# Last SwiGLU of a two-layer diffusion trunk on one core: two weight units multiply the residual sums before they are normalised

## The chip, the cores and the metric

One core of a Trainium2 chip runs the whole program. The metric is the device time of one execution in microseconds (us), the median over runs. Three runs of the kernel before stand at 1689.14, 1692.32 and 1695.26 us.

## The reference

Two layers work on 256 latent tokens and 256 context tokens of width 1024. Each layer is a half-step SwiGLU, a token mixer and another half-step SwiGLU. Every sub-layer scales and shifts its input by conditioning (adaLN), and every result is normalised after the residual sum:

```python
def mod_input(z, mm, slot):
    return z * (1.0 + mm[:, 3 * slot + 1]) + mm[:, 3 * slot]

def gated_post_norm(z, y, mm, slot, g, b):
    return layer_norm(DEEPNORM_ALPHA * z + mm[:, 3 * slot + 2] * y, g, b)

def swiglu(h, w1, w2):
    gate, up = jnp.split(h @ w1, 2, axis=-1)
    return (jax.nn.silu(gate) * up) @ w2
```

The mixer of the second (odd) layer is attention with 8 query heads. Behind it only the 256 latent tokens are needed, so the last SwiGLU works on 256 columns. This case is about the place between the two: output projection of the attention, layer norm, modulation, first product (w1) of the last SwiGLU. With z the residual sums, mu their mean over the features and r the inverse deviation, one column block of that product is sum over features of w * ((z - mu) * r * s + t), where s and t join the norm's gain and bias with the modulation. It can also be written as r * (w . (s z) - mu * (w . s)) + w . t, and this is what the change does for two blocks.

## The kernel before, in words

Features lie on the partitions in KC = 8 chunks of 128, tokens along the free axis. Every float32 product is made of three float32r products: weight and input are each split into a high and a low part, and high x high, low x high and high x low are added in one PSUM bank.

**Units.** The weights stream through the kernel as units of 128x1024 (512 KB), all numbered in one order. SyncE loads unit n into a ring of RING = 7 buffers `raw`, and may do so once TensorE has used up unit n - 6 (`load_unit`). ScalarE makes the high part in `w_hi` (`split_hi`, line 832; a ring of 6), VectorE the low part in `w_lo` (`split_lo`, line 1277), written over the raw buffer of the unit before. TensorE counts finished units in the semaphore `w_used`. ScalarE and VectorE have no queue of their own for this: where the program order puts `split_to(n)`, there all units up to n - 1 are split, in between their other work. Usually they are AHEAD = 4 units or so in front of TensorE.

**Output projection of the attention** (`odd_mixer`, eight units `o_out`). When TensorE has finished block c, VectorE adds it to the residual `hz` (line 1362) and adds the result to `sum1` (line 1373; for chunk 0 a copy, line 1370). ScalarE squares chunk c - 1 (line 891), and GpSimd adds the squares of chunks 1 to 6 to `sum2` (line 767). Both splitters split one unit per block in between.

**Norm 4** (`one_norm(4)`, that is `norm_sums` and `norm_spread`). TensorE turns `sum1` and `sum2` into one sum per token by products with one column (lines 2176, 2181, 2186) and spreads the sum of the residuals over all partitions in bank 5 (line 2189). VectorE makes the inverse deviation in fifteen small steps on two columns (`norm_step`, lines 1384 to 1411), the last two of which write it as a diagonal. TensorE spreads it in bank 4 (line 2195). Then VectorE goes chunk by chunk through `normalise`: `centre` (line 1420), `scale` (line 1429), and `lower` (line 1440), which makes the low part of the new input from what ScalarE has made in `apply_norm`: the high part `a_hi` (line 869) and the unrounded input `tmp_b` (line 872).

**First product of the last SwiGLU** (`ffn(3)`). 22 units make one half of the hidden width: a gate unit and an up unit for each of HH = 11 hidden steps; then come eight w2 blocks of two units, and the second half the same. Call the 22 units of the first half u0 to u21. Before, `first_four` (line 2230) takes u0 to u3 together, chunk by chunk as the input comes. The units behind are `paired_unit` (lines 2119 and 2120): high weight against both input parts in one product of 512 columns, then low weight against 256 columns. Unit u goes to one of banks 0 to 3 and waits (`bank_read`) until the unit four before it was read. In `hidden_step`, ScalarE applies SiLU to the gate (line 936, or 930 in a paired step, where lines 927 and 932 first copy the other half of the bank aside), VectorE multiplies (line 1530, or 1522 behind the adds of lines 1512 and 1516), ScalarE writes the high part (line 942) and VectorE the low part (line 1533). Line 881 (`keep`) scales the residual in between. A hidden step splits two units: one ahead of the product, one behind the high part.

Of the kernel before, what the change touches and what calls it, by code (L numbers as in the profile page):

```python
# [101 lines left out]
def paired_step(fi, half, j):  # L102

    return FFNS[fi][3] < T and (half == 1 or j >= 2)
# [124 lines left out]
def make_plan():  # L229
# [11 lines left out]
    def ffn(fi):  # L241
        layer, f = FFNS[fi][:2]
        for half in range(2):
            p.mark(("w1", fi, half))
            for j in range(HH):
                m = (fi * 2 + half) * HH + j
# [112 lines left out]
    "gate_rest", "gate_exp", "gla_ops", "hy_mid", "hy_read", "zf_ready", "att_even", "att", "att_read", "att_kept", "att_masked",  # L359
    "kst_turned", "kst_read", "ds", "ds_read", "state_ready", "g_read", "o_lower", "o_done", "o_sq",  # L360
    "o_root", "o_scaled", "o_turned", "gla_out", "z_turned", "zt_read",
    "dft", "dft_read", "spec_mixed", "spec_out", "skip_made", "idft", "idft_read", "cat", "cat_hi", "cat_ready",
# [7 lines left out]
def hybrid_trunk(nc, x_t, par_d, w1_d, w2_d, ada_d, ew_d, ev_d, eo_d, ow_d, ov_d, oo_d, gu_d,  # L370
# [4 lines left out]
    with ExitStack() as ctx:  # L375
# [108 lines left out]
        out_lo = [put(f"out_lo{i}", [P, UCOL], F32R, at=X + (52 + 4 * i) * K) for i in range(3)]  # L484
        osqr = put("osqr", [P, TC, GH * GDV], at=X + 56 * K)
# [261 lines left out]
        @block.gpsimd  # L747
        def _(pool):
            g = nc.gpsimd
            g.memset(scolp[:], 0.0).then_inc(s["zeroed"], 1)  # L750
            g.memset(ident[:], 0.0).then_inc(s["ones_made"], 1)
            pool.wait_ge(s["ones_made"], 1)
            g.affine_select(out=ident[:], in_=ident[:], compare_op=ALU.not_equal, fill=1.0, base=0,
                            pattern=[[-1, P]], channel_multiplier=1).then_inc(s["ones_made"], 1)
            g.memset(ones[:], 1.0).then_inc(s["ones_made"], 1)
            g.memset(fh[:], 1.0).then_inc(s["ones_made"], 1)

            def add_squares(m):
# [27 lines left out]
            pool.wait_ge(s["gate_rest"], 4)  # L786
# [11 lines left out]
        def _(act):  # L798
# [94 lines left out]

            def norm_inputs(m, nu):
# [24 lines left out]
            def ffn(fi):  # L919
                nt = FFNS[fi][3]  # L920

                def hidden_step(n, m, j):

                    act.wait_ge(s["w_used"], n + 1)
                    if paired_step(fi, half, j):
# [22 lines left out]
                for half in range(2):  # L948
# [5 lines left out]
                    for j in range(HH):  # L954
                        hidden_step(n0 + 2 * j, m0 + j, j)
# [53 lines left out]
            def even_mixer():  # L1009
# [17 lines left out]
                for e in range(4):  # L1027
                    act.wait_ge(s["gate_rest"], e + 1)
# [89 lines left out]
                for h in range(GH):  # L1118
# [3 lines left out]
                    A.copy(a_hi[:, YC + h, :], go[:, h, :]).then_inc(s["cat_hi"], 1)  # L1122
                for c in range(YC):
                    act.wait_ge(s["cat"], c + 1)
                    A.copy(a_hi[:, c, :], yt[:, c, :]).then_inc(s["cat_hi"], 1)
# [6 lines left out]
            def odd_mixer():  # L1132
# [121 lines left out]
        def _(dve):  # L1254
# [187 lines left out]

            def normalise(m, nu, j0):
# [40 lines left out]
                else:  # L1484
                    for i in range(NORM_STEPS):
                        norm_step(m, 0, i)
                    if m < 5:
                        split_to(nu + 4)
# [3 lines left out]
                    for c in range(KC):  # L1492
# [6 lines left out]
                        if m < 5 and c >= 1:  # L1499
                            lower(m, 0, c - 1)  # L1500
                    if m < 5:
                        lower(m, 0, KC - 1)

            def ffn(fi):
                _, _, _, nt, adas = FFNS[fi]

                def hidden_step(n, m, j, pieces):

                    if paired_step(fi, half, j):
# [8 lines left out]
                        if j < HH - 1:  # L1518
# [4 lines left out]
                                        ALU.mult).then_inc(s["hraw_ready"], 1)  # L1523
                    else:
# [14 lines left out]
                for half in range(2):  # L1539
# [12 lines left out]
                    for j in range(HH):  # L1552
                        hidden_step(n0 + 2 * j, m0 + j, j, pieces(j))
# [185 lines left out]
            def even_mixer():  # L1739
# [12 lines left out]
                for e in range(4):  # L1752
# [5 lines left out]
                    else:  # L1758
# [6 lines left out]
                                    ALU.subtract).then_inc(s["gate_rest"], 1)  # L1765
# [166 lines left out]
                def lower_cat(c, at, src):  # L1932

                    dve.wait_ge(s["cat_hi"], at + 1)
                    V.tensor_tensor(a_lo[:, c, :], src, a_hi[:, c, :].bitcast(F32), ALU.subtract)\
                        .then_inc(s["cat_ready"], 1)
# [43 lines left out]
            def odd_mixer():  # L1980
# [120 lines left out]
        def _(pe):  # L2101
# [160 lines left out]

            def paired_unit(n, j):
# [6 lines left out]
            def ffn(fi):  # L2270
                _, _, _, nt, adas = FFNS[fi]
                n_sub = SUB_OF_FFN[fi]
                for half in range(2):
                    n0, j0 = plan.base[("w1", fi, half)]
                    m0 = (2 * fi + half) * HH
                    if fi == half == 0:
                        pass
                    elif half == 0:
                        first_four(n_sub - 1, n0, j0, (0, 1)[:nt // SEQ])
# [7 lines left out]
                    for u in range(4, 2 * HH):  # L2287
# [180 lines left out]
            def even_mixer():  # L2468
# [188 lines left out]
                for pair in ((0, 1), (2, 3)):  # L2657
# [3 lines left out]
                    for at, k in enumerate(ks[:YC]):  # L2661
                        pe.wait_ge(s["cat_ready"], at + 1)
                        for u in pair:
                            four_out(k, u)
                for at, k in enumerate(ks[YC:KC - 2]):
                    pe.wait_ge(s["cat_ready"], YC + at + 1)
                    for u in range(4):
                        four_out(k, u)
                pe.wait_ge(s["cat_ready"], KC)
# [179 lines left out]
            one_norm(4)  # L2849
# [104 lines left out]
```

## Time and profile before

| | |
|---|---|
| runs, median (lowest to highest) | 1692.32 us (1689.14 to 1695.26) |
| the profiled execution's own time | 1695.77 us |
| its span | 1694.0 us |
| TensorE busy | 1667.0 us, 98% of the span |
| VectorE, ScalarE, GpSimd busy | 1182.8, 700.7, 72.7 us |
| last product of the attention's output projection | 1482.62 us |
| first product of the last SwiGLU | 1490.94 us |
| start of its first paired unit u4 | 1504.82 us |

Times within the trace are microseconds from the start of the span. The difference between the execution's own time and its span (1.77 us) lies around the span. In a view in order of time a row gives start, duration, engine, line, operation, tiles and, in square brackets, how long the engine stood idle before it and what released it. VectorE and ScalarE start an operation some 0.1 us before the one before it is shown as ended, so the cost of an operation in a queue is the distance between two starts.

### The profile page before, as it was taken

The page shows a single profiled execution, that of the slowest core. Times are in us where ns is not written, and L with a number is a line of the kernel's source. Part 1 is how long each engine was busy: PE and PEld are TensorE (multiplying, and loading weights), DVE is VectorE, ACT ScalarE, POOL GpSimd, SP SyncE. Part 2 cuts the span into 40 slices and gives each one's busy share as a digit, 9 for nine tenths or more (in the row PEclk, how much of TensorE's full clock was granted, in tenths as well). Part 3 has the DMA queues.
Part 4 walks back from the last instruction along what each step waited for, and adds up shares of the span by engine and source line. Part 5 has one row for each costly group of instructions (what it writes and reads, how often), then busy time and mean ns, then how long its engine had stood idle before and what let it go on. Part 6 is the DMA issues. An engine that isn't in the chain of part 4 may idle for free. (4 is left out here: it accounts for less than half of the span.)

```text
span 1694.0 us, 23629 instructions
## 1 busy us (share of the span) xinstructions
PE 1667.0 (98%) x9147; PEld 1404.5 (83%) x9147; DVE 1182.8 (70%) x1868; ACT 700.7 (41%) x1141; POOL 72.7 (4%) x62
## 2 busy tenths in 40 slices
PE   9999999999999999999999999999999999989997
PEld 6788888889877898888888898888888888878886
DVE  5577948978686866778533476778466687776767
ACT  3442242225645437422222246322323277665453
POOL 1000000001000020000000110000000110200001
PEclk9999999999999999999999999999999999989998
DMA  9665546632321232555322334554465342245653
GB/s 314 249 209 174 173 153 220 208 95 83 114 79 52 74 125 83 198 174 160 120 96 81 92 118 149 199 169 148 161 222 190 98 143 69 83 140 163 210 165 111
DMA packets 87094, 248.39 MB, mean 147 GB/s; under 512 B 8900, under 2 KB 24997, under 8 KB 86982
## 3 DMA queue, kind: packets, MB, share of 16 engines
q1 hardware_dynamic: 86504, 245.98, 44.8%
q8 instruction: 73, 1.20, 0.3%
q0 software_dynamic: 256, 0.46, 0.1%
q10 hardware_dynamic: 222, 0.43, 0.1%
q14 instruction: 39, 0.32, 0.1%
HBM read 245.79 MB, written 1.05 MB: 146 GB/s over the span
## 5 line engine op out<-in xcount | busy, mean ns | idle before, releaser
L1277 DVE TENSOR_TENSOR w_lo<-raw,w_hi 128x1024 fp32r<-128x1024 f32 (+2 forms) x337 | 380.5, 1129 | 154.9 <-ACT w_hi L832 148.3
L2104 PE MATMUL bank<-a_both,w_hi 128*128 128x512 f32 (+1 forms) x1200 | 462.2, 385 | 2.7 <-DVE w_lo L1277 1.4
L2105 PE MATMUL bank<-a_both,w_lo 128*128 128x512 f32 (+1 forms) x1200 | 460.2, 383 | 0.0
L2106 PE MATMUL bank<-a_both,w_hi 128*128 128x512 f32 (+1 forms) x1200 | 460.1, 383 | 0.0
L832 ACT CAST w_hi<-raw 128x1024 fp32r<-128x1024 f32 (+2 forms) x337 | 319.8, 955 | 161.0 <-DMA raw<-in_dram 157.7
L2104 PEld LDWEIGHTS bank<-a_both,w_hi 128*128 128x128 f32 x1200 | 225.5, 188 | 49.3 <-issue 2.3
L2106 PEld LDWEIGHTS bank<-a_both,w_hi 128*128 128x128 f32 x1200 | 225.5, 188 | 44.4
L2105 PEld LDWEIGHTS bank<-a_both,w_lo 128*128 128x128 f32 x1200 | 225.6, 188 | 43.8
L1295 DVE SCALAR_TENSOR_TENSOR acc<-ada,scol,acc 128x1024 f32<-128x1024 f32 x189 | 234.9, 1280 | 8.9 <-DMA ada<-in_dram 7.0
L2104 PE MATMUL bank<-h_both,w_hi 128*128 128x512 f32 (+1 forms) x473 | 183.5, 388 | 0.0
L2106 PE MATMUL bank<-h_both,w_hi 128*128 128x512 f32 (+1 forms) x473 | 182.9, 387 | 0.0
L2105 PE MATMUL bank<-h_both,w_lo 128*128 128x512 f32 (+1 forms) x473 | 182.8, 387 | 0.0
L942 ACT CAST h_both<-tmp_b 128x512 fp32r<-128x512 f32 (+1 forms) x88 | 49.9, 567 | 315.3 <-DVE tmp_b L1530 287.9
L1362 DVE SCALAR_TENSOR_TENSOR hz<-bank,acol,hz 128x256 f32<-128x256 f32 x136 | 61.3, 479 | 88.7 <-PE bank L2106 88.2
L767 POOL TENSOR_TENSOR sum<-sum,sq 128x256 f32<-128x256 f32 (+1 forms) x41 | 63.0, 1538 | 1339.4 <-ACT sq L891 1339.2
L2119 PE MATMUL bank<-a_both,w_hi 128*128 128x512 f32 x320 | 113.2, 399 | 0.0
L936 ACT ACTIVATE tmp_a<-bank 128x512 f32<-128x512 f32 (+1 forms) x68 | 40.1, 589 | 169.0 <-PE bank L2106 161.5
L2104 PEld LDWEIGHTS bank<-h_both,w_hi 128*128 128x128 f32 x473 | 88.8, 188 | 18.2
L2106 PEld LDWEIGHTS bank<-h_both,w_hi 128*128 128x128 f32 x473 | 88.8, 188 | 18.1
L2105 PEld LDWEIGHTS bank<-h_both,w_lo 128*128 128x128 f32 x473 | 88.8, 188 | 17.9
L1533 DVE TENSOR_TENSOR h_both<-tmp_b,h_both 128x512 fp32r<-128x512 f32 (+1 forms) x88 | 55.1, 626 | 55.7 <-ACT h_both L942 55.7
L1530 DVE TENSOR_TENSOR tmp_b<-tmp_a,bank 128x512 f32<-128x512 f32 (+1 forms) x68 | 46.1, 678 | 64.9 <-PE bank L2106 64.7
(338 smaller groups left out, 2248.6 us busy)
## 6 DMA issues: line engine op xcount, KB each, us to landing
raw<-in_dram SPq DMA_DIRECT2D x229, 512.0 KB, 3.8
ada<-in_dram SPq DMA_DIRECT2D x120, 512.0 KB, 3.9
raw<-in_dram SPq DMA_DIRECT2D x64, 384.0 KB, 3.3
raw<-in_dram SPq DMA_DIRECT2D x64, 320.0 KB, 2.9
first<-in_dram SPq DMA_DIRECT2D x32, 256.0 KB, 5.9
first<-in_dram SPq DMA_DIRECT2D x8, 512.0 KB, 10.4
hz<-in_dram SPq DMA_DIRECT2D x3, 512.0 KB, 8.4
out_dram<-hz SPq DMA_DIRECT2D x8, 128.0 KB, 1.7
```

Of the source, the lines that this page charges most:

```text
L767: g.tensor_tensor(sum2[:, cols], sum2[:, cols], sq[:, c % 2, cols], ALU.add).then_inc(s["s2_added"], 1)
L832: A.copy(hi_of(n)[:, 0:cols], raw[:, n % RING, 0:cols]).then_inc(s["hi_ready"], 1)
L942: A.copy(h_hi[:, j, 0:nt], tmp_b[:, m % 2, 0:nt]).then_inc(s["hhi_ready"], 1)
L1277: V.tensor_tensor(lo_of(n)[:, 0:cols], raw[:, n % RING, 0:cols], hi_of(n)[:, 0:cols].bitcast(F32), ALU.subtract).then_inc(s["lo_ready"], 1)
L1295: ins = V.scalar_tensor_tensor(acc[:, w, cols], ada[:, p % 2, :], scol[:, w, k:k + 1], acc[:, w, cols], ALU.mult, ALU.add)
L1362: ins = V.scalar_tensor_tensor(hz[:, c, cols], jbank(j)[:, cols], acol[:, m, w, 2, c:c + 1], hz[:, c, cols], ALU.mult, ALU.add)
L1530: V.tensor_tensor(tmp_b[:, m % 2, 0:nt], tmp_a[:, m % 2, 0:nt], jbank(j0 + n - n0 + 1)[:, 0:nt], ALU.mult).then_inc(s["hraw_ready"], 1)
L1533: V.tensor_tensor(h_lo[:, j, 0:nt], tmp_b[:, m % 2, 0:nt], h_hi[:, j, 0:nt].bitcast(F32), ALU.subtract).then_inc(s["h_ready"], 1)
L2104: pe.matmul(dst, w_at(0), x_at(0), start=first, stop=False, skip_group_check=shared)
L2105: pe.matmul(dst, w_at(1), x_at(0), start=False, stop=False, skip_group_check=shared)
L2106: return pe.matmul(dst, w_at(0), x_at(1), start=False, stop=last, skip_group_check=shared)
L2119: pe.matmul(out, w_at(0), both[:, :, k, 0:SEQ], start=first, stop=False, skip_group_check=True)
```

## The change

The program order of the norm's and the product's parts is rewritten around the first three hidden steps of the last SwiGLU's first half:

- u0 and u1 (hidden step 0) are multiplied with `zu` instead of the normalised input: ScalarE makes its high part, s times `hz`, one operation a chunk (`unscaled_hi`), and VectorE its low part (`unscaled_lo`), while the output projection still runs. Two more columns hold -s/1024 and t, so each product has 258 columns. They go to banks 6 and 7.
- TensorE (`six_units`) does nine of those 48 products ahead of the norm's sums, 24 between the sums and the spreading of the deviation, and 15 behind it. Then u2 and u3 take the chunks as they come, and u4 and u5 follow two and four chunks behind them. u4 and u5 are no longer paired.
- Hidden steps are taken in the order 1, 2, 0, 3, ... Step 0 makes mean and deviation good on VectorE in seven operations ahead of the last one, reads banks 4 to 7, and holds no unit's split.
- The splits move: that of u3 goes ahead of the norm's steps, those of u4 and u5 go into the chunk loop of `normalise` on VectorE (behind chunks 1 and 3), and ahead of `apply_norm` on ScalarE.
- Some semaphores get other names and are shared (`cat_hi` is `cast_hi`, `cat_ready` is `cast_lo`, `gate_rest` is `gate_in`), which changes nothing in the even layer's order.

```diff
 def paired_step(fi, half, j):
-    return FFNS[fi][3] < T and (half == 1 or j >= 2)
+    return FFNS[fi][3] < T and (half == 1 or j >= 3)
+
+def step_order(fi, half):
+    return [1, 2, 0, *range(3, HH)] if FFNS[fi][3] < T and half == 0 else [*range(HH)]
...
+            def unscaled_hi(c):
+                if c == 0:
+                    act.wait_ge(s["mod_cols"], 5)
+                    A.activation(zu[:, 0, :, SEQ:SEQ + 1], acol[:, 5, 0, 0, :].rearrange("p (k o) -> p k o", o=1),
+                                 ACT.Copy, scale=-1.0 / D)
+                    A.copy(zu[:, 0, :, SEQ + 1:SEQ + 2], acol[:, 5, 0, 1, :].rearrange("p (k o) -> p k o", o=1))
+                A.activation(zu[:, 0, c, 0:SEQ], hz[:, c, 0:SEQ], ACT.Copy, scale=acol[:, 5, 0, 0, c:c + 1])\
+                    .then_inc(s["cast_hi"], 1)
...
                 else:
+                    if m < 5:
+                        split_to(nu + 4)
                     square_z(m, KC - 1)
                     if m < 5:
-                        split_to(nu + 4)
+                        unscaled_hi(KC - 1)
+                        split_to(nu + 6)
                         for c in range(KC):
                             apply_norm(m, 0, c)
...
+                    elif j == 0 and nt < T:
+                        act.wait_ge(s["gate_in"], 5)
+                        A.activation(tmp_a[:, m % 2, 0:nt], tmp_a[:, m % 2, 0:nt], ACT.Silu, bias=lift[:, 0, 1:2])\
+                            .then_inc(s["silu_ready"], 1)
...
                     split_to(first_unit("o_out") + c + 4)
                     if c > 0:
                         square_z(4, c - 1)
+                        unscaled_hi(c - 1)
...
+            def unscaled_lo(c):
+                dve.wait_ge(s["cast_hi"], KC + c + 1)
...
+                V.scalar_tensor_tensor(zu[:, 1, c, 0:SEQ], hz[:, c, 0:SEQ], acol[:, 5, 0, 0, c:c + 1],
+                                       zu[:, 0, c, 0:SEQ].bitcast(F32), ALU.mult, ALU.subtract).then_inc(s["cast_lo"], 1)
...
                 else:
+                    if m < 5:
+                        split_to(nu + 4)
                     for i in range(NORM_STEPS):
                         norm_step(m, 0, i)
                     if m < 5:
-                        split_to(nu + 4)
+                        unscaled_lo(KC - 1)
...
                             lower(m, 0, c - 1)
+                        if m < 5 and c in (1, 3):
+                            split_to(nu + 5 + c // 2)
...
+                    elif j == 0 and nt < T:
+                        dve.wait_ge(s["w_used"], n + 2)
+                        for g in range(2):
+                            V.tensor_copy(lift[:, g, :], bank[6 + g][:, SEQ:SEQ + 2])
+                        ins = V.tensor_copy(total_z[:], bank[5][:, 0:SEQ])
+                        link(ins)
+                        for g, room in enumerate((tmp_a, tmp_b)):
+                            out = room[:, m % 2, 0:nt]
+                            link(V.scalar_tensor_tensor(out, total_z[:], lift[:, g, 0:1], bank[6 + g][:, 0:SEQ],
+                                                        ALU.mult, ALU.add))
+                            ins = V.tensor_tensor(out, out, bank[4][:, 0:SEQ], ALU.mult)
...
+                        V.scalar_tensor_tensor(out, out, lift[:, 1, 1:2], tmp_a[:, m % 2, 0:nt], ALU.add, ALU.mult)\
+                            .then_inc(s["hraw_ready"], 1)
...
                 for c in range(KC):
                     split_to(first_unit("o_out") + c + 4)
+                    if c == KC - 1:
+                        unscaled_lo(c - 1)
                     sum_z(4, c, first_job("o_out") + c)
+                    if 0 < c < KC - 1:
+                        unscaled_lo(c - 1)
...
+            def six_units(m, n0, j0):
+                def unscaled(u, k):
+                    def part(lhs, rhs):
+                        return pe.matmul(bank[6 + u][:, 0:SEQ + 2], w_tile(n0 + u, k)(lhs), zu[:, rhs, k, :],
+                                         start=(k == lhs == rhs == 0), stop=(k == KC - 1 and rhs == 1))
...
+                unit_split(n0 + 1)
+                for k in range(3):
+                    unscaled(0, k)
+                norm_sums(m, 0)
+                for k in range(3, KC - 1):
+                    unscaled(0, k)
+                for k in range(4):
+                    unscaled(1, k)
+                norm_spread(m, 0)
+                for k in range(4, KC - 1):
+                    unscaled(1, k)
+                for u in range(2):
+                    unscaled(u, KC - 1).then_inc(s["w_used"], 1)
...
+                for k in range(KC):
+                    pe.wait_ge(s["ahi_ready"], input_at(m + 1, 0, k))
+                    for u in (2, 3):
+                        part(u, k, 0, 0)
+                        part(u, k, 1, 0)
+                    if k >= 2:
+                        whole(4, k - 2)
+                    if k >= 4:
+                        whole(5, k - 4)
+                    pe.wait_ge(s["a_ready"], input_at(m + 1, 0, k))
+                    for u in (2, 3):
+                        ins = part(u, k, 0, 1)
...
-            one_norm(4)
             ffn(3)
```

## Rows read from the trace of the kernel before

**Rows 1.** The page: busy time, share of the span, instructions of each engine.

```profile
PE 1667.0 (98%) x9147; PEld 1404.5 (83%) x9147; DVE 1182.8 (70%) x1868; ACT 700.7 (41%) x1141; POOL 72.7 (4%) x62
```

**Rows 2.** Table by stage: length, PE PEld DVE ACT POOL busy, clock, DMA, GB/s.

```profile
1485.90:1490.94 5.04, 1.22 (x2) 0.50 (x2) 4.65 (x17) 0.65 (x2) 0.00 (x0) 0.50 0.00 2
1490.94:1495.90 4.96, 4.96 (x23) 4.96 (x24) 4.17 (x12) 4.49 (x9) 0.00 (x0) 0.50 0.00 0
1495.90:1504.82 8.92, 8.92 (x75) 8.92 (x75) 4.17 (x9) 6.40 (x12) 0.00 (x0) 0.99 0.21 62
...
1505.00:1535.00 30.00, 30.00 (x171) 26.00 (x171) 22.65 (x34) 22.33 (x41) 0.00 (x0) 1.00 0.67 213
```

**Rows 3.** TensorE in order of time, around norm 4.

```profile
1482.62 0.28 PE L2106 MATMUL bank<-a_both,w_hi 128*128 128x256 f32 x1
...
1483.93 0.61 PE L2181 MATMUL bank<-ones,sum 128*128 128x1 f32 x4 [0.54 <-DVE sum L1373]
...
1488.12 1.22 PE L2195 MATMUL bank<-sq,ones 128*128 128x256 f32 x2 [2.60 <-DVE sq L1411]
1490.94 0.58 PE L2230 MATMUL bank<-a_both,w_hi 128*128 128x256 f32 x1 [1.60 <-ACT a_both L869]
...
1504.82 0.42 PE L2119 MATMUL bank<-a_both,w_hi 128*128 128x512 f32 x1
...
1510.50 0.40 PE L2119 MATMUL bank<-a_both,w_hi 128*128 128x512 f32 x1
```

**Rows 4.** VectorE in order of time: last sums, norm steps, first chunks.

```profile
1480.06 0.49 DVE L1362 SCALAR_TENSOR_TENSOR hz<-bank,acol,hz 128x256 f32<-128x256 f32 x1 [0.71 <-PE bank L2106]
...
1480.92 1.22 DVE L1277 TENSOR_TENSOR w_lo<-raw,w_hi 128x1024 fp32r<-128x1024 f32 x1
1482.93 0.48 DVE L1362 SCALAR_TENSOR_TENSOR hz<-bank,acol,hz 128x256 f32<-128x256 f32 x1 [0.79 <-PE bank L2106]
1483.45 0.42 DVE L1373 TENSOR_TENSOR sum<-sum,hz 128x256 f32<-128x256 f32 x1
1485.02 0.16 DVE L1384 TENSOR_SCALAR stat<-bank 128x2 f32<-128x2 f32 x1 [1.15 <-PE bank L2186]
...
1487.98 1.22 DVE L1277 TENSOR_TENSOR w_lo<-raw,w_hi 128x1024 fp32r<-128x1024 f32 x1
1489.12 0.75 DVE L1420 SCALAR_TENSOR_TENSOR tmp_a<-bank,hz 128x256 f32<-128x256 f32 x2
1489.78 0.41 DVE L1429 TENSOR_TENSOR hz<-tmp_a,bank 128x256 f32<-128x256 f32 x1
...
1491.49 0.42 DVE L1440 TENSOR_TENSOR a_both<-tmp_b,a_both 128x256 fp32r<-128x256 f32 x1 [0.62 <-ACT tmp_b L872]
1491.83 0.42 DVE L1420 SCALAR_TENSOR_TENSOR tmp_a<-bank,hz 128x256 f32<-128x256 f32 x1
```

**Rows 5.** ScalarE in order of time: the first chunk.

```profile
1490.29 0.60 ACT L869 ACTIVATE a_both<-hz,acol 128x256 fp32r<-128x256 f32 x1 [5.49 <-DVE hz L1429]
1490.80 0.58 ACT L872 ACTIVATE tmp_b<-hz,acol 128x256 f32<-128x256 f32 x1
```

**Rows 6.** GpSimd in order of time: the last sum of squares.

```profile
1481.08 1.66 POOL L767 TENSOR_TENSOR sum<-sum,sq 128x256 f32<-128x256 f32 x1 [1.13 <-ACT sq L891]
```

**Rows 7.** ScalarE and VectorE in order of time: the second hidden step.

```profile
1505.99 0.38 ACT L936 ACTIVATE tmp_a<-bank 128x256 f32<-128x256 f32 x1
1506.26 1.04 ACT L832 CAST w_hi<-raw 128x1024 fp32r<-128x1024 f32 x1
...
1508.59 0.42 DVE L1530 TENSOR_TENSOR tmp_b<-tmp_a,bank 128x256 f32<-128x256 f32 x1
...
1509.04 0.41 ACT L942 CAST h_both<-tmp_b 128x256 fp32r<-128x256 f32 x1 [1.24 <-DVE tmp_b L1530]
```

**Rows 8.** Table by stage of TensorE alone, another place with little work.

```profile
522.50:525.00 2.50, 1.06 (x16) 1.00 0.01 3
```

**Rows 9.** TensorE: plain float32 products of 256 columns, two instructions each.

```profile
1460.14 1.89 PE L2799 MATMUL bank<-pt,vo 128*128 128x256 f32 x8
```

More of the change, by code:

```diff
@@ L245, in ffn @@
             for j in range(HH):
-                m = (fi * 2 + half) * HH + j
+                m = (fi * 2 + half) * HH + step_order(fi, half).index(j)
                 for g in range(2):
@@ L484, in hybrid_trunk @@
         out_lo = [put(f"out_lo{i}", [P, UCOL], F32R, at=X + (52 + 4 * i) * K) for i in range(3)]
+        zu = put("zu", [P, 2, KC, SEQ + 2], F32R, at=X + 4 * K)
+        total_z = put("total_z", [P, SEQ], at=X + 22 * K)
+        lift = put("lift", [P, 2, 2], at=X + 21 * K)
         osqr = put("osqr", [P, TC, GH * GDV], at=X + 56 * K)
@@ L953, in ffn @@
                     split_to(n0 + AHEAD)
-                    for j in range(HH):
-                        hidden_step(n0 + 2 * j, m0 + j, j)
+                    for at, j in enumerate(step_order(fi, half)):
+                        hidden_step(n0 + 2 * j, m0 + at, j)
                     for oc in range(SPLIT_FROM[m] if half else KC):
@@ L1523, in hidden_step @@
                                         ALU.mult).then_inc(s["hraw_ready"], 1)
+                    elif j == 0 and nt < T:
[9 more added lines that the diff above has]
+                            ins = V.tensor_tensor(out, out, bank[4][:, 0:SEQ], ALU.mult)
+                            if g == 0:
+                                ins.then_inc(s["gate_in"], 1)
+                            else:
+                                link(ins)
+                        dve.wait_ge(s["silu_ready"], m + 1)
+                        V.scalar_tensor_tensor(out, out, lift[:, 1, 1:2], tmp_a[:, m % 2, 0:nt], ALU.add, ALU.mult)\
+                            .then_inc(s["hraw_ready"], 1)
                     else:
@@ L1551, in ffn @@
                     split_to(n0 + AHEAD)
-                    for j in range(HH):
-                        hidden_step(n0 + 2 * j, m0 + j, j, pieces(j))
+                    for at, j in enumerate(step_order(fi, half)):
+                        hidden_step(n0 + 2 * j, m0 + at, j, pieces(j))
                         for x in turns(j):
@@ L1932, in lower_cat @@
                 def lower_cat(c, at, src):
[L1934 removed]
+                    dve.wait_ge(s["cast_hi"], at + 1)
                     V.tensor_tensor(a_lo[:, c, :], src, a_hi[:, c, :].bitcast(F32), ALU.subtract)\
[L1936 removed]
+                        .then_inc(s["cast_lo"], 1)
                 for c in range(YC - 1):
@@ L2261, in first_four, with part, whole @@
                         ins.then_inc(s["w_used"], 1)
+            def six_units(m, n0, j0):
[3 more added lines that the diff above has]
+                                         start=(k == lhs == rhs == 0), stop=(k == KC - 1 and rhs == 1))
+                    pe.wait_ge(s["cast_hi"], KC + k + 1)
+                    part(0, 0)
+                    part(1, 0)
+                    pe.wait_ge(s["cast_lo"], KC + k + 1)
+                    return part(0, 1)
+                def part(u, k, lhs, rhs):
+                    return pe.matmul(jbank(j0 + u)[:, 0:SEQ], w_tile(n0 + u, k)(lhs), tokens(A_IN, k, SEQ)(rhs),
+                                     start=(k == lhs == rhs == 0), stop=(k == KC - 1 and rhs == 1))
+                def whole(u, k):
+                    if k == 0:
+                        unit_split(n0 + u)
+                        bank_read(pe, j0 + u - 4)
+                    part(u, k, 0, 0)
+                    part(u, k, 1, 0)
+                    return part(u, k, 0, 1)
+                unit_split(n0 + 1)
[12 more added lines that the diff above has]
+                for u in (2, 3):
+                    unit_split(n0 + u)
+                    bank_read(pe, j0 + u)
+                for k in range(KC):
+                    pe.wait_ge(s["ahi_ready"], input_at(m + 1, 0, k))
+                    for u in (2, 3):
+                        part(u, k, 0, 0)
+                        part(u, k, 1, 0)
+                    if k >= 2:
[3 more added lines that the diff above has]
+                    pe.wait_ge(s["a_ready"], input_at(m + 1, 0, k))
+                    for u in (2, 3):
+                        ins = part(u, k, 0, 1)
+                        if k == KC - 1:
+                            ins.then_inc(s["w_used"], 1)
+                for k in range(KC - 2, KC):
+                    ins = whole(4, k)
+                ins.then_inc(s["w_used"], 1)
+                for k in range(KC - 4, KC):
+                    ins = whole(5, k)
+                ins.then_inc(s["w_used"], 1)
@@ L2277, in ffn @@
                         pass
+                    elif half == 0 and nt < T:
+                        six_units(n_sub - 1, n0, j0)
                     elif half == 0:
-                        first_four(n_sub - 1, n0, j0, (0, 1)[:nt // SEQ])
+                        first_four(n_sub - 1, n0, j0, (0, 1))
                     else:
@@ L2286, in ffn @@
                                 paired_unit(n0 + u, j0 + u)
-                    for u in range(4, 2 * HH):
+                    for u in range(6 if half == 0 and nt < T else 4, 2 * HH):
                         bank_read(pe, j0 + u)
@@ L2665, in even_mixer @@
                 for at, k in enumerate(ks[YC:KC - 2]):
-                    pe.wait_ge(s["cat_ready"], YC + at + 1)
+                    pe.wait_ge(s["cast_lo"], YC + at + 1)
                     for u in range(4):
                         four_out(k, u)
-                pe.wait_ge(s["cat_ready"], KC)
+                pe.wait_ge(s["cast_lo"], KC)
                 for u in range(4):
```

21 lines of the change are left out of this document (13 added, 8 removed).

## The prediction

> **What bounds the kernel now.** The page comes first: TensorE is busy for 1667.0 of 1694.0 us [rows 1], so time can only come from its 27 idle us or from its clock. The table by stage shows where both are lost together: from 1485.90 to 1490.94 TensorE has 1.22 us of work and its granted clock is 0.50, and the next 4.96 us are full of work at the same 0.50. From 1505 on it works without a gap at clock 1.00 [rows 2]. So what is gained ahead of the paired units reaches the end whole, if those units then find their operands. The order of time on TensorE names the waits: 0.54 us for the last residual sum, 2.60 us for the inverse deviation, 1.60 us for the first normalised chunk, 4.74 us in all [rows 3]. With the half clock (below) some 7.5 us can be had; the stretch can give no more.
>
> **Prices on TensorE.** At full clock 75 float32r products of 256 columns take 8.92 us, 0.12 us each; at half clock 23 take 4.96 us, 0.216 us each [rows 2]. The half clock so costs 23 x 0.096 = 2.2 us, and some 0.6 us in the spreading of the deviation (1.22 us shown [rows 3]; I take half). Two paired units, 16 pairs, take 1510.50 - 1504.82 = 5.68 us [rows 3], 2.84 each; unpaired they are 24 x 0.12 = 2.88 each, so u4 and u5 get 0.1 us dearer.
>
> No row has 258 columns. The bounds are 0.12 us (float32r, 256 columns) and what plain float32 pays: eight instructions for four products, (1.89 - 0.38) / 7 = 0.215 us each with 0.38 taken as the first one's own latency, 0.43 us a product [rows 9]. I take 0.12, the row of the same type and nearly the same width, and keep 0.43 for a rival. The Trainium skill, TensorE: Matmul & The Clock Gate, section Back-to-back issue gap, puts the distance of two products at the column count over 2.4 GHz plus 2.5 ns; by that rule two columns more would cost 48 x 0.8 ns = 0.04 us in all, an estimate that changes nothing.
>
> **Step 1, VectorE ahead of the norm.** Nearest to `unscaled_lo` is `lower`, with two SBUF inputs and a float32r output of the same size: it starts at 1491.49, the next at 1491.83, so 0.34 us [rows 4]. The lower bound is what hides, nothing; the upper the 0.52 us from one residual sum to its follower (1482.93 to 1483.45 [rows 4]), which is inflated by a wait. Seven of them and two tiny ones ahead of the last sum make 2.6 us. They use up VectorE's idle 0.71 and 0.79 us ahead of the last two sums [rows 4], and about 0.3 us of smaller gaps; the last sum moves from 1482.93 to about 1483.75. ScalarE's new part is eight scalings, between 0.32 and 0.60 us each ([rows 5] for the second); it is busy for little over half of this stretch and I cost them at nothing. If that cover were gone, the squares would come late.
>
> **Step 2, TensorE meanwhile.** Its last projection product starts at 1482.62 [rows 3]. Nine unscaled products fill 1482.74 to 1483.8, then it waits 0.9 us for the sum (residual sum to released product was 1.0 us: 1482.93 to 1483.93). The statistics reach VectorE at about 1485.85, 0.8 us later than the 1485.02 of before [rows 4].
>
> **Step 3, the norm's chain.** Before, the fifteen steps ran from 1485.02 to 1487.98, then u3's split cost 1.14 us ahead of the first `centre` at 1489.12 [rows 4]. Now this split lies ahead of the steps, while TensorE sums, and is hidden; the last `unscaled_lo`, 0.34 us, takes its place. 1485.85 + 2.96 + 0.34 = 1489.15: the first chunk comes when it came before, 1490.3 [rows 5]. The gain is not there. It is that TensorE does the other 39 products meanwhile: sums to 1486.1, 24 products (2.9 us) to 1489.0, spreading 0.5 us, 15 products (1.8 us) to 1491.3. Two units are then done that before had not begun, at full clock.
>
> **Step 4, the chunk loop.** u2 to u5 need 96 x 0.12 = 11.5 us. VectorE's two splits now sit in this loop, 1.14 us each. Chunk 0 is lowered at 1491.5 as before, the split of u4 follows from 1491.85 to 1493.0, and chunk 1 is lowered only after another centre and scale, at 1493.65 to 1494.1. TensorE, with 0.72 us of work for chunk 0 and 0.48 for the high part of chunk 1, is there at 1492.5: it waits 1.6 us. The split of u5 behind chunk 2 costs it 1.1 us in the same way; from chunk 4 on u4 and u5 give it more work than the loop's pace. 1491.3 + 11.5 + 1.6 + 1.1 + 0.1 = 1505.6 for the end of u5.
>
> **Step 5, what is late next: the splits.** u6 must be split inside hidden step 1, and ScalarE's SiLU stands ahead of it in its queue, waiting for u2, which ends together with u3 at 1503.4. SiLU 0.27, high part 1.04, low part 1.2, product 0.42 to free the bank [rows 7]: u6 starts at 1506.5, 0.9 us after TensorE was ready. Before, it started at 1510.50 [rows 3]: 4.0 us gained here. Then step 0 comes third. It holds no split, but VectorE's seven small and middle operations (two of 0.1, one of 0.35, four of 0.45 to 0.5, by the starts of [rows 4] with a wait between) and the last product make about 2.8 us ahead of the high part, and the splits of u10 and u11 stand behind. u8 and u9 are split in step 2, by 1513.1; step 0 lasts to 1516.8; u10's high part is written at 1516.6 to 1517.7 and its low part by 1518.95. TensorE wants u10 at 1506.5 + 4 x 2.84 = 1517.85 and gets it at about 1519.1: 1.3 us lost. From there on a step costs VectorE and ScalarE less than TensorE's 5.68 us and they catch up. The loads are no matter: u6 can be issued when u0 is used up, now at 1491 instead of about 1502, into a queue that moves nothing then [rows 2], and SyncE's order has only weights.
>
> **Sum.** -4.0 + 1.3 = -2.7 us. The profiled execution took 1695.77 us and would take 1693.1; it lies 3.45 us above the median of the three runs, so against the median of 1692.32 the forecast is 1689.6 us. This kernel's measurement can tell about 0.3%, 5.1 us, from no change; most outcomes lie within it.
>
> **GpSimd.** Its last add of squares starts at 1481.08 and takes 1.66 us, ending 0.6 us after VectorE's split of 1480.92 to 1482.14 [rows 4, 6]. It looks as if it waited for that split. The Trainium skill, SBUF — State Buffer, section SBUF: two separate sides, says that VectorE with two SBUF inputs and GpSimd exclude each other for a whole instruction; the trace agrees with that. In the new order this add's square is ready at 1482.2, the split lasts to 1483.2, `unscaled_lo` to 1483.6, then comes a sum from PSUM: it would end at 1484.2, before the 1484.7 when the last sum is there, and cost nothing.
>
> **Rivals.** (a) *The splits are not late.* If ScalarE and VectorE come through steps 1, 2 and 0 faster than I reckon, up to 0.9 + 1.3 us come back: -4.9 us, 1687.4; with a shorter chunk loop -6, 1686.3. For it: TensorE found no late split before, though u5's was ready just in time. Against: the order in the code. Chance 0.18, half of it beyond 5.1 us. (b) *The clock falls all the same.* The sums still make a poor stretch, 0.9 us of waiting and 1.4 us of products with one column, and two more waits follow. It would cost 0.096 x 23 to 40 products, 2.2 to 3.8 us: 1691.8 to 1693.4, no change. Against: from 522.50 to 525.00 TensorE had 1.06 us of work in 2.5 us and kept clock 1.00 [rows 8]; before, it fell only in the 2.60 us wait. Chance 0.12. (c) *GpSimd's add loses to the split of u3 as well* and ends at 1486.4; the sums start 1.7 us later and the gain shrinks to 0.6 to 1: 1691.5. By the row above it goes in at the PSUM sum. Chance 0.06. (d) *Slower: 258 columns run at the pace of plain float32.* Place: `six_units`, 48 products. Price 48 x 0.31 = 14.9 us, of which 2.7 us fill the waits of step 4 and 0.4 us others: -2.7 + 11.8 = +9 us, 1701.4. It decides from 0.23 us a product (no gain) and makes the kernel slower by 0.3% from 0.34. Chance 0.04. (e) *The splits are late for longer:* each step after 0 starts from a debt, up to the 3 us of step 0: +0 to +2 us, 1692 to 1694. Chance 0.12.
>
> **Numbers.** Forecast 0.48 for -1.5 to -4.5 us, 1687.8 to 1690.8. Faster by over 0.3%: half of (a), plus 0.09 for what the sum undersizes and for the spread of the medians, 0.18. Slower: (d) and a bit of (e), 0.05. The rest, 0.77, within 0.3%. The range of 1685.0 to 1695.0 takes in (a), (b), (c), (e) and some of the 6 us between the runs, and leaves out (d).
>
> **What would show it.** TensorE: 24 products without a gap between the sums and the spreading, clock 1.00 throughout; waits near chunk 1 and chunk 3 of 1.6 and 1.1 us; u6 behind the low part of its split or the bank's product, 0.9 us; u10 behind its split, 1.3 us; no wait later. VectorE: last residual sum 0.8 us late, first `centre` at the same distance from the projection's end as before. A clock of 0.50 before the final norm, 258-column products over 0.13 us apart, or TensorE idle in u12 to u21 would make it wrong.

## The result and the profile of the changed kernel

The change makes the kernel slower. Twenty runs of it have a median of 1697.56 us, twenty of the kernel before 1693.21 us; the ratio is 1.0021 (95% interval 1.0015 to 1.0027). Measured again later it was 1.0010 (1.0002 to 1.0019). The forecast was 1689.6 us, 2.7 us under the 1692.32 us that three runs of the kernel before had as their median. The profiled execution took 1697.57 us, with a span of 1695.8 us.

From here on times are given as distances from the last product of the attention's output projection, which starts at 1482.62 us before and at 1481.82 us in the changed kernel; what lies ahead of it is the same work.

| distance from the last projection product, us | before | forecast | changed |
|---|---|---|---|
| last residual sum starts on VectorE | 0.31 | 1.1 | 4.48 |
| first of the fifteen norm steps | 2.40 | 3.2 | 6.70 |
| spreading of the deviation starts | 5.50 | 6.4 | 11.32 |
| u6 starts | 27.88 | 23.9 | 28.92 |
| u10 starts (before: four units of 2.825 behind u6) | 39.2 | 36.5 | 41.70 |

At u10 the changed kernel is 2.5 us behind in this execution. Behind it TensorE waits for nothing up to the final norm, so these 2.5 us are lost here. That the medians lie 4.35 us apart is taken up with the last runs.

First the table by stage (columns as in [rows 2]) for the changed kernel:

```profile
1481.94:1488.30 6.36, 3.12 (x23) 2.68 (x22) 6.29 (x9) 3.62 (x7) 0.95 (x2) 0.98 0.28 88
1488.30:1491.50 3.20, 3.20 (x14) 3.02 (x15) 2.60 (x17) 1.20 (x2) 0.00 (x0) 0.51 0.00 0
1491.50:1495.90 4.40, 4.40 (x36) 4.26 (x35) 2.63 (x9) 1.61 (x4) 0.00 (x0) 1.00 0.00 0
```

In the first 6.36 us TensorE is busy for 3.12, while VectorE has 6.29 us of work: VectorE sets the pace here. Then comes a row of 3.2 us with the granted clock at half (0.51, that is 1.2 GHz), before it comes back; in windows of 0.5 us the half clock lasts 3.4 us, from about 1488.05. TensorE in order of time shows what it waited for; it answers to [rows 3]:

```profile
1483.12 0.39 PE L2331 MATMUL bank<-zu,w_hi 128*128 128x258 f32 x1 [1.02 <-DVE w_lo L1303]
...
1484.95 0.61 PE L2239 MATMUL bank<-ones,sum 128*128 128x1 f32 x4 [0.49 <-POOL sum L775]
...
1487.29 0.61 PE L2244 MATMUL bank<-ones,sum 128*128 128x1 f32 x4 [1.73 <-DVE sum L1399]
...
1491.61 0.40 PE L2331 MATMUL bank<-zu,w_hi 128*128 128x258 f32 x2
...
1491.96 0.40 PE L2331 MATMUL bank<-zu,w_hi 128*128 128x258 f32 x2
...
1493.14 0.59 PE L2258 MATMUL bank<-sq,ones 128*128 128x256 f32 x2
...
1498.10 0.69 PE L2341 MATMUL bank<-a_both,w_hi 128*128 128x256 f32 x3 [1.16 <-DVE a_both L1466]
...
1501.55 0.69 PE L2341 MATMUL bank<-a_both,w_hi 128*128 128x256 f32 x3 [0.79 <-DVE a_both L1466]
...
1510.74 0.50 PE L2182 MATMUL bank<-a_both,w_hi 128*128 128x512 f32 x1 [0.72 <-DVE tmp_b L1589]
...
1523.52 0.47 PE L2182 MATMUL bank<-a_both,w_hi 128*128 128x512 f32 x1 [1.22 <-DVE w_lo L1303]
```

The last four waits were foretold (1.6, 1.1, 0.9 and 1.3 us), the first three add up to 3.24 us and were forecast as 0.9. Between 1491.61 and 1491.96 lie three products: 0.117 us each with 258 columns. The cause of the early waits stands on VectorE and GpSimd, in the loop over the output projection:

```profile
1474.18 0.47 DVE L1388 SCALAR_TENSOR_TENSOR hz<-bank,acol,hz 128x256 f32<-128x256 f32 x1
1474.69 0.43 DVE L1399 TENSOR_TENSOR sum<-sum,hz 128x256 f32<-128x256 f32 x1
1475.03 0.48 DVE L1477 SCALAR_TENSOR_TENSOR zu<-hz,acol,zu 128x256 fp32r<-128x256 f32 x1
1475.43 1.76 DVE L1303 TENSOR_TENSOR w_lo<-raw,w_hi 128x1024 fp32r<-128x1024 f32 x1
1477.11 0.47 DVE L1388 SCALAR_TENSOR_TENSOR hz<-bank,acol,hz 128x256 f32<-128x256 f32 x1
...
1486.30 0.47 DVE L1388 SCALAR_TENSOR_TENSOR hz<-bank,acol,hz 128x256 f32<-128x256 f32 x1
```

```profile
1475.18 0.92 POOL L775 TENSOR_TENSOR sum<-sum,sq 128x256 f32<-128x256 f32 x1 [2.00 <-ACT sq L899]
```

The split `w_lo` takes 1.76 us, where it took 1.22 before [rows 4], and GpSimd's add takes 0.92 us, where it took 1.66 [rows 6]. The two have changed places. Before, the split was already running when the add was asked for, and the add waited. Now `unscaled_lo` stands between the residual sum and the split; the square is ready while it runs, GpSimd is next, and the split waits until GpSimd's add ends at 1476.10. From there to the split's end at 1477.19 is 1.09 us, about what a split costs from its start to the next one's (1.14 us in [rows 4]).

### The profile page after: what moved, and what is told of

It is laid out like the page before. It is cut to its first block and busy times, and to the rows that moved or that the text cites. A ratio compares the mean times of both kernels' runs of the same rounds, so it can differ in the third digit from the quotient of the medians.

```text
span 1695.8 us, 23684 instructions
## 1 busy us (share of the span) xinstructions
PE 1666.5 (98%) x9163; PEld 1405.2 (83%) x9163; DVE 1190.9 (70%) x1883; ACT 702.7 (41%) x1149; POOL 68.2 (4%) x62
## 5 line engine op out<-in xcount | busy, mean ns | idle before, releaser
L775 POOL TENSOR_TENSOR sum<-sum,sq 128x256 f32<-128x256 f32 (+1 forms) x41 | 58.7, 1432 | 1349.0 <-ACT sq L899 1348.9
L2182 PE MATMUL bank<-a_both,w_hi 128*128 128x512 f32 x304 | 107.7, 399 | 1.9 <-DVE w_lo L1303 1.2
```

Source lines behind the costliest of these rows:

```text
L2182: pe.matmul(out, w_at(0), both[:, :, k, 0:SEQ], start=first, stop=False, skip_group_check=True)
```

## The experiments

Each kernel was timed in five rounds against the kernel before on the same chip. Line numbers differ by one or two between them.

**Scaling ahead of squaring.** One swap on ScalarE asks GpSimd 0.4 us later.

```diff
                     if c > 0:
-                        square_z(4, c - 1)
+                        act.wait_ge(s["z_ready"], z_count(4, c - 1, 0))
                         unscaled_hi(c - 1)
+                        square_z(4, c - 1)
```

> ScalarE scales chunk c for the unscaled product before it squares it, in the loop over the output projection; nothing else changes. Theory (the port between VectorE and GpSimd): GpSimd's add is now asked for 0.4 us later, when the split of the next unit is already under way, so it waits for the split instead of holding it up. The six splits of 1.76 us become 1.22 us, GpSimd's adds grow from 0.92 to about 1.6 us, the last residual sum comes about 3 us earlier relative to the last projection product (before it was 4.5 us behind it, expected 1.5), and the kernel is 2.5 to 3.5 us faster than the changed kernel, ratio to before 0.9995 to 1.0010. Rival (VectorE is only over-full, or the split is slowed by ScalarE's cast on the same buffers): splits stay at 1.76 us, time as the changed kernel, ratio about 1.0021.

Median 1692.52 us, ratio 0.9989 (0.9980 to 0.9998). VectorE's splits (first) and GpSimd's adds (second) in the views of their source lines, shortest, median and longest in ns:

```profile
L1304 DVE TENSOR_TENSOR w_lo<-raw,w_hi x9: 1210/1214/1226, 1463.3 to 1485.2; 128x1024 fp32r<-128x1024 f32 x9
```

```profile
L775 POOL TENSOR_TENSOR sum<-sum,sq x6: 1684/1688/1826, 1470.3 to 1482.5; 128x256 f32<-128x256 f32 x6
```

and the same two groups in the changed kernel:

```profile
L1303 DVE TENSOR_TENSOR w_lo<-raw,w_hi x8: 1210/1758/1768, 1467.0 to 1487.1; 128x1024 fp32r<-128x1024 f32 x8
```

```profile
L775 POOL TENSOR_TENSOR sum<-sum,sq x6: 742/922/931, 1469.2 to 1484.0; 128x256 f32<-128x256 f32 x6
```

GpSimd's add is now the one that grows, from 0.92 to 1.69 us, and no split is long any more. The last residual sum starts at a distance of 1.85 instead of 4.48 us, and u10 at 37.70 instead of 41.70: 4.0 us from one swapped pair of lines. That is somewhat more than was expected (2.5 to 3.5 us, and a ratio of 0.9995 to 1.0010): 2.6 us are the sum's, and the clock stays up too, as the table by stage (1.00) shows:

```profile
1484.00:1495.00 11.00, 8.97 (x66) 8.37 (x67) 9.88 (x32) 5.34 (x10) 0.16 (x1) 1.00 0.33 112
```

**Short adds.** GpSimd's six adds for norm 4 get two columns. The kernel so leaves out the squares of chunks 1 to 6 for the other 254 tokens, and its deviation is another number; it serves to time the order alone.

```diff
+                        if m == 4:
+                            cols = slice(0, 2)
                         g.tensor_tensor(sum2[:, cols], sum2[:, cols], sq[:, c % 2, cols],
                                         ALU.add).then_inc(s["s2_added"], 1)
```

> GpSimd's six adds of squares for norm 4 work on 2 of the 256 columns (the sums of squares of chunks 1 to 6 are left out, so the deviation of norm 4 is another number). Port theory: all splits of the loop at 1.22 us, the unscaled low part of chunk 0 at 0.48 instead of 1.01 us, last residual sum within 1.3 us of the last projection product, 3 to 3.5 us faster than the changed kernel, a little more than with the scaling first. Rival (over-full VectorE or ScalarE's cast): splits stay at 1.76 us and time stays.

Median 1691.26 us, ratio 0.9976 (0.9966 to 0.9986). Splits:

```profile
L1305 DVE TENSOR_TENSOR w_lo<-raw,w_hi x8: 1217/1219/1222, 1467.1 to 1483.9; 128x1024 fp32r<-128x1024 f32 x8
```

ScalarE's casts and VectorE's own operations are all still there, so neither an over-full VectorE nor the cast made the splits long. The last sum starts at 1.24 us. The forecast had reckoned with 1.1: its arithmetic was nearly right for a VectorE without GpSimd beside it.

**Low parts ahead of the sums.** The blocked operation should change with the order, if the port is what blocks.

```diff
-                    if c == KC - 1:
+                    if c > 0:
                         unscaled_lo(c - 1)
                     sum_z(4, c, first_job("o_out") + c)
-                    if 0 < c < KC - 1:
-                        unscaled_lo(c - 1)
```

> The changed kernel, but VectorE makes the unscaled low part of chunk c-1 ahead of the sum of chunk c (so behind the split) for every c, not for the last alone; GpSimd is asked right behind the sum, when the split has begun. Port theory: splits go back to 1.22 us, but GpSimd's add then takes the port as the split ends and holds up the unscaled low part instead, about 0.95 instead of 0.48 us each; the last sum stays over 3.5 us behind the last projection product and the time stays near the changed kernel, ratio 1.0010 to 1.0025. Rival (the split alone is slow, by ScalarE's cast on its buffer): low parts stay at 0.48, the sum comes 3 us sooner, ratio 0.999.

Median 1696.39 us, ratio 1.0008 (0.9999 to 1.0017), a little under the range expected. VectorE in order of time:

```profile
1474.80 1.22 DVE L1303 TENSOR_TENSOR w_lo<-raw,w_hi 128x1024 fp32r<-128x1024 f32 x1
1475.93 0.96 DVE L1477 SCALAR_TENSOR_TENSOR zu<-hz,acol,zu 128x256 fp32r<-128x256 f32 x1
1476.82 0.47 DVE L1388 SCALAR_TENSOR_TENSOR hz<-bank,acol,hz 128x256 f32<-128x256 f32 x1
```

The split is back at 1.22 us and the low part behind it has grown from 0.48 to 0.96 us. The last sum starts at 4.11 us, nearly as late as in the changed kernel. So the same half microsecond is paid each time by whichever operation with two SBUF inputs comes when GpSimd's turn is. In the kernel before and with the scaling first, the operation behind the split is the residual sum out of PSUM, and it pays nothing.

**First split waited for alone.**

```diff
-                unit_split(n0 + 1)
+                unit_split(n0)
                 for k in range(3):
                     unscaled(0, k)
                 norm_sums(m, 0)
                 for k in range(3, KC - 1):
                     unscaled(0, k)
+                unit_split(n0 + 1)
```

> TensorE waits for u0's split ahead of its first nine unscaled products and for u1's only ahead of u1's first. Theory: the wait of 1.02 us for u1's split ahead of the first unscaled product goes, but TensorE then waits as much longer for the last residual sum, which it does not set: below 0.3 us gained. Rival: the idle second is what lets the clock fall in the sums, and without it the products between the sums and the spreading run at 0.12 instead of 0.216 us, 1.5 to 2.5 us gained.

Median 1696.25 us, ratio 1.0009 (1.0000 to 1.0018). The changed kernel itself, measured again, had 1.0010, so nothing is gained. The wait of 1.02 us is gone and the next one grew from 0.49 to 1.77 us:

```profile
1485.25 0.61 PE L2239 MATMUL bank<-ones,sum 128*128 128x1 f32 x4 [1.77 <-POOL sum L775]
1487.58 0.61 PE L2244 MATMUL bank<-ones,sum 128*128 128x1 f32 x4 [1.73 <-DVE sum L1399]
```

In this execution the clock was at half for 6.8 of the 7 us in the row below (mean 0.54), and u6 came at 30.48, later than in the changed kernel's (28.92). So the gain that the rival promised did not come. But the idle second was moved and not removed: ahead of the one-column products TensorE still waits 3.50 us in all, against 3.24. The run shows that it does not matter for the clock where the second lies, and leaves open whether the idle time as a whole lets it fall.

```profile
1487.50:1494.50 7.00, 6.92 (x32) 6.74 (x33) 4.83 (x20) 2.30 (x4) 0.00 (x0) 0.54 0.00 0
```

**Deviation spread after 12 products.** `norm_spread(m, 0)` is put ahead of u1's first product.

```diff
+                norm_spread(m, 0)
-                for k in range(4):
-                    unscaled(1, k)
-                norm_spread(m, 0)
-                for k in range(4, KC - 1):
+                for k in range(KC - 1):
                     unscaled(1, k)
```

> The deviation is spread after 12 unscaled products (u0 chunks 3 to 6) instead of 24; the other 12 follow behind it. Theory: VectorE's wait of 1.14 us for the spreading goes, the chunk loop begins 1.1 us sooner while TensorE has 27 products left to cover it, and its two waits for lowered chunks (1.16 and 0.79 us) shrink; 0.8 to 1.8 us faster than the changed kernel. Rival: the deviation is not ready that early (it was ready 0.1 us after the 12th product would end at the slow clock), TensorE stands idle for it, and nothing is gained.

Median 1695.32 us, ratio 1.0008 (0.9999 to 1.0017). The spreading starts at 9.85 instead of 11.32 us, TensorE's wait for chunk 1 is gone, that for chunk 3 is 0.80 us as it was, and u6 starts at 27.55: 1.4 us gained by the trace, as the theory had it, against an execution with half clock for the same 3.4 us. The times (1.0008 beside 1.0010 and 1.0021 for the changed kernel) allow it but do not prove it.

**Step 0 as the sixth.** On top of the scaling first.

```diff
-    return [1, 2, 0, *range(3, HH)] if FFNS[fi][3] < T and half == 0 else [*range(HH)]
+    return [1, 2, 3, 4, 5, 0, *range(6, HH)] if FFNS[fi][3] < T and half == 0 else [*range(HH)]
```

> Scaling first (as the kernel that was faster) and hidden step 0 as the sixth instead of the third, where the splits are two units ahead. Theory: u10's wait of 1.22 us goes and no other comes in its place; about 1.2 us faster than with the scaling first alone, ratio to before 0.9980 to 0.9985. Rival: the debt of step 0 only moves, and a unit around u16 waits 1 us or more.

Median 1692.07 us, ratio 0.9991 (0.9982 to 0.9999). By the trace the theory holds: TensorE's last wait ahead of the final norm is u6's, and u10's 1.22 us is gone; no unit behind waits instead. The ratio is above the range expected (0.9980 to 0.9985) and does not show the 1.2 us against the kernel with the scaling first alone (0.9989, on another chip); both intervals are wide enough for it, so the gain rests on the trace alone.

**Splits ahead of the hidden steps.** On top of that, on ScalarE and VectorE:

```diff
-                    split_to(n0 + AHEAD)
+                    split_to(n0 + (7 if nt < T and half == 0 else AHEAD))
```

> As the kernel with step 0 sixth, and both splitters also split u4 to u6 ahead of the first hidden step, so that u6's split no longer stands behind the SiLU that waits for u2. Theory: u6's wait of 0.73 us goes or shrinks to the wait for its bank (below 0.3 us); 0.5 to 0.8 us faster. Rival: the bank of u6 is read only behind the product of hidden step 1, which sets the same time, and the wait stays above 0.5 us.

Median 1690.96 us, ratio 0.9982 (0.9973 to 0.9991). u6 starts at 24.02 instead of 24.91 us, without a wait.

**Low part of chunk 6 behind the last sum.** On top of that, with u1's split waited for at u1:

```diff
-                    if c == KC - 1:
-                        unscaled_lo(c - 1)
                     sum_z(4, c, first_job("o_out") + c)
-                    if 0 < c < KC - 1:
+                    if c > 0:
                         unscaled_lo(c - 1)
```

> As the kernel before it in this call, and the unscaled low part of chunk 6 is made behind the last residual sum, under which GpSimd's last add can run, and TensorE waits for u1's split only ahead of u1. Theory: the last sum comes 0.8 us sooner (1.85 to about 1.0 us behind the last projection product), the statistics 0.5 us, and the kernel gains 0.3 to 0.7 us: ratio to before 0.9970 to 0.9980. Rival: the first low part of the norm then stands ahead of the split of u3 and of the steps and takes all of it back.

Median 1689.22 us, ratio 0.9971 (0.9961 to 0.9982). With the scaling first, the one low part that still stood right behind a split was chunk 6's, and it was the one that was held up:

```profile
1482.36 1.21 DVE L1304 TENSOR_TENSOR w_lo<-raw,w_hi 128x1024 fp32r<-128x1024 f32 x1
1483.50 0.95 DVE L1478 SCALAR_TENSOR_TENSOR zu<-hz,acol,zu 128x256 fp32r<-128x256 f32 x1
1484.37 0.47 DVE L1389 SCALAR_TENSOR_TENSOR hz<-bank,acol,hz 128x256 f32<-128x256 f32 x1
```

In the new order the sum out of PSUM follows the split, and everything costs its own time:

```profile
1480.09 1.21 DVE L1304 TENSOR_TENSOR w_lo<-raw,w_hi 128x1024 fp32r<-128x1024 f32 x1
1481.22 0.47 DVE L1389 SCALAR_TENSOR_TENSOR hz<-bank,acol,hz 128x256 f32<-128x256 f32 x1
1481.73 0.44 DVE L1400 TENSOR_TENSOR sum<-sum,hz 128x256 f32<-128x256 f32 x1
1482.09 0.47 DVE L1478 SCALAR_TENSOR_TENSOR zu<-hz,acol,zu 128x256 fp32r<-128x256 f32 x1
```

The last sum starts at 0.97 us, u6 at 23.46, and the only waits left between the projection and the final norm are 0.33 us for GpSimd and the two in the chunk loop (1.15 and 0.80 us).

**Both once more, on one chip.**

> The changed kernel itself once more, on the same chip as the next. By its trace u10 starts 2.5 us later behind the last projection product than before, which is 0.15% of the time; the first measurement was 1.0021 (1.0015 to 1.0027). The theory that all of it lies in this stretch expects 1.0010 to 1.0020; a loss elsewhere would keep it at 1.0021 or above.

> The best version once more (scaling first, step 0 sixth, u4 to u6 split ahead of the hidden steps, the low part of chunk 6 behind the last sum, u1's split waited for at u1). Its trace puts u10 4.4 us earlier than before: ratio 0.9970 to 0.9978, and 0.0040 below the changed kernel.

The changed kernel: median 1696.79 us, ratio 1.0010 (1.0002 to 1.0019). The best version: 1690.40 us, ratio 0.9976 (0.9967 to 0.9985), so it beats both kernels, the changed one by 6.4 us on this chip (0.0034 between the ratios, where 0.0040 was expected). In this execution of the changed kernel all waits of TensorE are the same as in the first to 0.02 us, but u6 started at 30.48 instead of 28.92 us, because half clock lasted longer, 6.8 us (from about 1488.4 to 1495.2) instead of 3.4:

```profile
1489.60:1493.00 3.40, 3.40 (x16) 3.22 (x16) 2.98 (x16) 0.48 (x1) 0.00 (x0) 0.50 0.00 0
1493.00:1496.00 3.00, 3.00 (x17) 2.95 (x17) 0.51 (x3) 0.00 (x0) 0.00 (x0) 0.63 0.00 0
```

So at u10 the changed kernel has lost 2.5 us in one execution and 4.1 us in another. The second is not the longer one, though (1696.79 against 1697.57 us). Behind u10 it takes 169.4 us where the first takes 172.3, with the granted clock at 1.00 in both: between 1560 and 1600 us TensorE runs 233 products in the second and 229 in the first, and between 1540 and 1545 us the pairs of products of its paired units start 0.346 us apart against 0.353. Up to u10 their distance was the same in both. The execution of "First split waited for alone" is the same again, 6.8 us of half clock and 169.3 us behind u10. No run shows why the pace differs. With equal pace (172.2 us behind u10 in the profiled execution of the kernel before) the loss is 2.5 us, or 1.0015 as a ratio, which is the lower end of the first measured interval and lies within the second. The 4.35 us between the medians are more because the profiled execution of the kernel before, 1695.77 us, lies 2.6 us above its median, while that of the changed kernel lies on its own; what those 2.6 us are is not shown.

## Why the prediction was wrong

- **The step that failed is "Step 1, VectorE ahead of the norm", together with the paragraph "GpSimd".** It said that seven low parts at 0.34 us and two tiny operations would use up VectorE's idle time and move the last sum to about 1483.75 (1.1 us behind the last product). They start 0.40 us apart rather than 0.34, which is 0.4 us in all. The rest is the port: the low part of chunk 0 took 1.01 instead of 0.48 us and five splits 1.76 instead of 1.22 us, 0.53 + 5 x 0.54 = 3.2 us. The measured distance is 4.48 us, 3.4 us more than forecast. Moving GpSimd's request (4.48 to 1.85 us) and shortening its adds (to 1.24) each took most of it away.
- **The prediction's own rows had the order.** It put the last square at 1482.2, some 0.2 us behind the start of the split that "lasts to 1483.2". By [rows 4, 6] the add is asked for 1.02 us behind the start of `hz` (1480.06 to 1481.08), and the split starts 0.86 us behind it (1480.92), 1.20 with a low part of 0.34 ahead of it. So the add comes first, by 0.2 us. Measured: 1.00 us for the add (1474.18 to 1475.18), 1.25 for the split.
- The prediction had the rule and used it in one direction. The Trainium skill, SBUF — State Buffer, section SBUF: two separate sides, says that whichever starts first gets the port for its whole instruction and the other is fully blocked. I asked only how long GpSimd would wait for VectorE. The runs show the other direction: the split 1.76 us with GpSimd ahead of it, 1.22 without, and 0.96 against 0.48 us for the low part. The trace agrees with the rule there too. Rival (c) was near, but it let GpSimd lose, once; GpSimd won, six times (chunk 0's low part and five splits).
- **Step 2 and the clock.** With the sum 3.4 us late TensorE stood idle for 3.24 us instead of 0.9 around its one-column products, and the granted clock fell to 0.50 before the 24 products. Behind the first of them the other 23 took from 1489.55 to 1493.14, 3.6 us where 0.12 us each would make 2.8. So rival (b), with a chance of 0.12, came true. It looks like a consequence of the late sum: in the six profiles of the new order in which the sum came within 1.9 us the granted clock was 1.00 throughout, in the five in which it came later than 4 us it fell to 0.50 every time. No run keeps the sum late and the clock up, or the other way round, so the link is not shown by itself.
- **Step 3** held where it was not moved: u3's split was hidden behind TensorE's sums, the steps took 2.96 us, and the chain shifted whole. One more cost was missed: at half clock the spreading stood behind 24 products while the deviation was ready, and VectorE waited 1.14 us for it.
- **Step 4** was right in kind and too large: 1.16 and 0.79 us for 1.6 and 1.1.
- **Step 5** was right: 0.72 us at u6 for 0.9 (u6 waits until the product of hidden step 1, `tmp_b`, has read its bank), 1.22 at u10 for 1.3 behind its low part, nothing later. The rival that they would not come, (a), fell. Each goes when its cause is moved: u10's with step 0 sixth, u6's with the splits ahead.
- **Prices on TensorE** were right: 0.117 us with 258 columns, so rival (d) fell, and full clock takes u2 to u5 at 0.12 us each product.
- **The sum.** Forecast at u10: 2.7 us earlier than before; measured: 2.5 us later. Of the 5.2 us between them, 4.0 went with the swap of scaling and squaring. Of the other 1.2 us, 0.7 are the sum that still came late there (1.85 for 1.1); the rest is not assigned.

## What to carry to other kernels

When an operation is slipped into VectorE's order, ask who else is waiting for its port, and who comes first now: an add on GpSimd that always stood behind a long VectorE operation can come ahead of it, and then it holds up the critical queue at every turn. The cure is order, not less work: let GpSimd's request come when the long operation is running and let an operation that reads PSUM follow it. Price a helper of half a microsecond in both directions before taking it as hidden.

## What the runs showed of the hardware

The port between VectorE and GpSimd costs the loser the rest of the winner's instruction, in either direction: GpSimd's add of 256 float32 columns takes 0.74 us at the least (at the turn where it holds up a low part) and 1.69 us behind a split; the split 1.22 us or 1.76, a low part 0.48 or 0.95 to 1.01. A VectorE operation with one input in PSUM and one in SBUF (`hz`) took 0.47 to 0.49 us in every one of these runs, also beside a running add. What I had not expected is that a single program order keeps the same loser for the whole loop, without a change of turns. The half clock of the changed kernel at this one place lasted 3.4 us in one execution and 6.8 us in another, with waits of TensorE that were the same to 0.02 us; and at a granted clock of 1.00 the pace of TensorE was not the same either, 229 or 233 products in 40 us, for a reason that no run shows.
